# Two attention stages of a fused Trainium2 kernel: scores issued first in a block, one product piece per block, taps moved behind

## Chip, cores, metric

The kernel runs on one core of a Trainium2 chip. The metric is the device time of one execution in microseconds (us). The engines are TensorE (PE), VectorE (DVE), ScalarE (ACT), GpSimd (POOL) and SyncE (SP), which issues most transfers.

## What is computed

A first block (hybrid attention, then a recurrent mixer, each with a feed-forward network) and a second one of two layers, over 512 tokens of width 1024. The change touches the attentions. The first has eight heads of dilated attention (units 0 to 3, two heads each) and four heads of differential attention (units 4 to 7), whose output is normalized per head:

```
attn = p[:, :, 0] - lam * p[:, :, 1]
return jnp.einsum('bhqk,bkhe->bqhe', attn, vf)
...
ob = rms_norm(ob, b_sub_norm) * (1.0 - lam_init)
```

A layer of the second block has four branches over one input projection: chunked attention with a table of relative positions (units 0 and 1), attention over latents with rotary positions (units 2 and 3), attention with a forget gate, whose logits get `F[t] - F[s]`, a running sum over the tokens (units 4 and 5), and a causal depthwise convolution of 31 taps over 256 channels, followed by a layer norm. The gated sum of the four branches goes into the output projection.

## The kernel before, in words

All weights come as 470 slabs of 128x1024 f32. SP fetches a slab into a ring of three (`fetch`), ACT rounds it to `w_hi` (L841), POOL subtracts for `w_lo` (L1829), and TensorE makes each product of three passes: high by high, low by high, high by low (L395 to L397). A slab is 24 such matmuls of 128x512. An operand made on the chip is split in the same way: ACT takes the high half (L889), DVE the low half (`take_low`, L1250).

The attention runs in blocks of 128 queries, four to a unit, numbered n through the units. A block is taken through these steps: `scores` (PE L459, two lanes, banks 0 and 1), the min over the shifted scores (DVE L1323), the exponential (`rise`, ACT L896), the weighing by the reciprocal of the sum (`weigh`, DVE L1333 and L1345; in units 4 to 7 with lambda, L1340), `turn` (PE transposes, L472), `unturn` (the turned tile copied back, ACT L886 or DVE L1352), and per unit `mix` (PE L489, weighted values). In the first attention, units 4 to 7 end with `submean` and `subnorm` (reciprocal L1459, a product, high and low half).

Every engine walks the same list of steps, which `attention_steps` writes (L259 to L293) once for the first attention (`steps0`) and once for the layers of the second (`steps2`). An engine takes its part of each step in the list's order; semaphores hold it where its input isn't there. In iteration n the list has, in this order: turn, mix if a unit is complete, unturn (all of block n−3, `LAG` at L22), a unit's end, the fill for n, score of block n, weighing of block n−1, the second fill for n. The fill is product work of other parts: in the first attention the query and key units (`qk`) and value units (`vb`), each of two 24-matmul pieces of 256 columns (`token_unit`, L498), and the first output products (`out`); in the second the latents, the d inputs, keys, values and queries of the latent attention, the heads of the forget attention and the gated products (`fill2`, L336, and the lists behind it). The second fill holds the taps of the convolution (c = 0 on DVE at L1744, c = 1 on ACT and POOL) and the forget gate's steps, from the gather and back through several transfers to `sums`, a scan over the tokens (L1731), a sign (L1733) and eight small transfers into the tile `aug` (L1999 and L2000). Block 16's score waits for the last of these:

```
                                if a % NB == 0:
                                    T.wait_ge(scaled, ("c_head", L, 4 + c))
                                    T.wait_ge(scaled, ("c_head", L, 6 + c))
                                    T.wait_ge(l_aug, L)
```

The latents' norm is a root, a reciprocal of 128x512 (L1670), a product (L1677) and the halves (`latent_parts`); the rotary step is `rope` (L1680 on). A part 1 of the latents belongs to keys and values, a part 0 of two slabs to the queries. Behind the attention come gated products with the convolution's mean, variance and norm among them (`conv`, from L1768 on DVE).

Of the kernel before, what the change touches and what calls it, by code (L numbers as in the profile page):

```python
# [11 lines left out]
ALU = mybir.AluOpType  # L12
ACT = mybir.ActivationFunctionType

P = 128
# [5 lines left out]
NPAIR = 3  # L21
LAG = 3  # L22
# [97 lines left out]
def program(nc, x_in, small_in, fixed_in, heads_in, rel_in, pos_in, out):  # L120
# [3 lines left out]
    with ctx:  # L124
# [125 lines left out]
        y = {}  # L250
# [8 lines left out]
        def attention_steps(stage, units, fill=(), vfill=(), extra=None):  # L259
            n_blocks = NB * units  # L260
            at_block, after_block = {}, {}
            for lists, where in ((fill, at_block), (vfill, after_block)):
                for items, n0, n1 in lists:
                    for i, item in enumerate(items):
                        where.setdefault(n0 + i * (n1 - n0) // len(items), []).append(item)
# [24 lines left out]
            for i, stage_ in enumerate(later):  # L290
                steps += (extra or {}).get(n_blocks + LAG + i, [])
                steps.append(stage_)
# [8 lines left out]
        def turn_bank(stage, n, k):  # L301
# [6 lines left out]
        vb_banks = {(0, 0): 6, (0, 1): 6, (1, 0): 5, (1, 1): 6}  # L308
        before0 = {19: [("vb", (0, 0))], 21: [("qk_turn", 7), ("vb", (0, 1))], 23: [("vb", (1, 0))], 25: [("vb", (1, 1))],
                   1: [("qk_turn", 2)], 2: [("qk", (3, 1))], 0: [("qk", (3, 0))], 3: [("qk_root", 3)]}  # L310
        for p in range(4, 8):
            n = 4 * p - 12
            before0[n] = [("qk", (p, 0))]
            before0[n + 1] = [("qk_turn", p - 1)]
            before0[n + 2] = [("qk", (p, 1))]
            before0.setdefault(n + 3, []).insert(0, ("qk_root", p))
        norm0 = [[("qk_norm", p)] for p in range(3, 8)]
        out_banks = (5, 6, 0, 1, 2, 3, 4, 7)
        early0 = {27: [(0, 0, 4)], 28: [(1, 0, 4)], 29: [(0, 4, 5), (1, 4, 5)], 31: [(0, 5, 6), (1, 5, 6)],
                  32: [(2, 0, 4)], 33: [(3, 0, 4)], 34: [(2, 4, 6), (3, 4, 6)],  # L320
                  35: [(o, 6, 7) for o in range(4)] + [(4, 0, 7)], 36: [(5, 0, 7)]}
        for n, v in early0.items():
            before0[n] = [("out", a) for a in v]
        steps0 = attention_steps("first", 8, vfill=[(norm0[p - 3], 4 * p - 9, 4 * p - 8) for p in range(3, 8)], extra=before0)

        def qk_ready(n):
# [5 lines left out]
        mixed_list = [f for pair in zip([("forget", f) for f in forget], tap_list) for f in pair] + tap_list[len(forget):36]  # L332
        mixed_list = [f for f in mixed_list if f != ("forget", None)]
        fill2 = ([("latents", 0), ("d_input", 0), ("latent_norms", 0), ("d_input", 1), ("latent_parts", 1), ("rope", 0)]
                 + [("b_key", h) for h in range(4)] + [("latent_parts", 0), ("b_values", 0)]
                 + [("b_query", h) for h in range(4)])  # L336
        c_heads = {4: 1184, 6: 1440, 5: 1312, 7: 1568}
        steps2 = attention_steps("second", 6, [
            (fill2, 0, 8), ([("c_head", n) for n in (4, 6, 5, 7)], 8, 16),
            ([("gated", (0, c)) for c in range(8)], 16, 24), ([("gated", (1, c)) for c in range(4)], 24, 27)],  # L340
            [(mixed_list, 8, 16), (tap_list[36:], 16, 26)])
# [23 lines left out]
        def tensor(T):  # L365
# [132 lines left out]
            def token_unit(key, bank, c0, blocks, m):  # L498
# [5 lines left out]
                first = place[name, 0][0]  # L504
                wait_bank(bank)
                for b in blocks:
                    o = banks[bank][:, 256 * (b % 2):256 * (b % 2) + 256]
                    cols = slice(P * b, P * b + P)
                    for k in range(8):
                        slab, at = place[name, k]  # L510
                        wh, wl = w_hi[:, slab % NPAIR, at:at + 256], w_lo[:, slab % NPAIR, at:at + 256]
                        rh, rl = xr[k]
                        T.wait_ge(w_low, slab)
                        T.wait_ge(low, ("x", m, k))
                        pe.matmul(o, rh[:, cols], wh, start=(k == 0), stop=False)  # L515
                        pe.matmul(o, rl[:, cols], wh, start=False, stop=False)  # L516
                        last = pe.matmul(o, rh[:, cols], wl, start=False, stop=(k == 7))  # L517
                        done = [key] if b == blocks[-1] and k == 7 else []
                        if b == 3 and (name, k) in closes:
                            done.append(("slab", slab))  # L520
                        if done:
                            last.then_inc(*product.tick(*done))

            def qk(p, i):
                kind, half = pairs[p]
                bank = pair_banks[p][i]
                token_unit(("qk", p, i), bank, (0, 512, 1536, 2048)[kind] + 256 * half, (2 * i, 2 * i + 1), 0)
                free[bank] = (scaled, ("qk", p, i))
# [26 lines left out]
            for p, i in ((0, 0), (0, 1), (1, 0)):  # L555
                qk(p, i)
            qk_turn(0)
            qk(1, 1)
            qk(2, 0)
            qk_turn(1)  # L560
            qk(2, 1)
# [8 lines left out]
            for what, a in steps0:  # L570
# [4 lines left out]
                elif what == "vb":  # L575
                    half, i = a
                    bank = vb_banks[a]
                    token_unit(("vb",) + a, bank, 2560 + 256 * half, (2 * i, 2 * i + 1), 0)
                    free[bank] = (vec, ("vb",) + a)
# [82 lines left out]
            def hybrid(L):  # L662
# [29 lines left out]
                for what, a in steps2:  # L692
                    if what == "latents":
                        for n, c0 in enumerate([768, 896, 1024]):
                            bk = plain(("latent", L, n), c0)
                            free[bk] = (scaled, ("latent", L, n))
# [45 lines left out]
                    elif what == "d_input":  # L742
                        for half, c0 in ((0, 1956), (1, 2212)):
                            bk = plain(("d", L, a, half), c0 + P * a)
                            free[bk] = (vec, ("d", L, a)) if half == 0 else (act, ("d", L, a))
# [43 lines left out]

                T.wait_ge(taps, ("conv", L, 0, 30))  # L790
                T.wait_ge(pool, ("conv", L, 1, 30))
                wait_bank(4)
                sum_over(4, ("conv_mean", L), one256, [dcon[:, 0, :], dcon[:, 1, :]])
                free[4] = (vec, ("centred", L, 1))
                gated(1, 4)
                gated(1, 5)
                for c in range(2):
                    T.wait_ge(squared, ("conv", L, c))
                wait_bank(0)
                sum_over(0, ("conv_var", L), one256, [tmp[:, 1, :], tmp[:, 2, :]])  # L800
                free[0] = (rooted, ("conv", L))
                for c in range(6, 8):
                    gated(1, c)
                for c in range(8):
                    gated(2, c)
# [26 lines left out]
        def scalar(A):  # L832
# [89 lines left out]
            def qk(p, i):  # L922

                unit_weights(("qk", p), i)
# [29 lines left out]
            qk(0, 0)  # L954
            qk(0, 1)
            qk_root(0)
            qk(1, 0)
            qk_turn(0)
            qk(1, 1)
            qk_root(1)  # L960
            qk(2, 0)
            qk_turn(1)
            qk(2, 1)
            qk_root(2)
            for what, a in steps0:
# [6 lines left out]
                elif what == "vb":  # L972
                    half, i = a
                    unit_weights(("vb", half), i)
                    A.wait_ge(product, ("vb",) + a)
                    copy(att[:, 20 + 2 * i, 256 * half:256 * half + 256], banks[vb_banks[a]][:, 0:256],
                         ("vb",) + a, scale=rtok[:, 2 * i:2 * i + 1])
# [125 lines left out]
            def hybrid(L):  # L1103
# [18 lines left out]
                for what, a in steps2:  # L1122
                    if what == "latents":
                        for n in range(3):
# [971 lines left out]
```

## Time and profile before

| | |
|---|---|
| runs, median of 3 | 2961.24 us (2959.28 to 2962.02) |
| the profiled execution | 2963.23 us |
| its span on the page | 2961.4 us |
| PE busy | 2830.0 us, 96% |
| DVE, ACT, POOL busy | 1330.2, 1210.9, 1231.8 us (45, 41, 42%) |
| first attention | about 44 to 303 us |
| second attention, layer 0 and 1 | about 1331 to 1600 and 2161 to 2432 us |

The page gives the busy time of each engine and the granted clock of TensorE in slices. The views used below are the table of windows (busy time of each engine in a stretch, with the mean granted clock), the table of waits (an engine and line, the line it waited for), and the timeline of one engine's instructions.

### The profile page before, as it was taken

How to read it: one execution, taken by the hardware profiler on the slowest of the kernel's cores; microseconds unless marked ns; L12 is line 12 of the kernel's file. 1: busy time of each engine (PE TensorE's matmuls, PEld its weight loads, DVE VectorE, ACT ScalarE, POOL GpSimd, SP SyncE). 2: the span in 40 equal slices, each digit the busy share in tenths (PEclk: the TensorE clock that was granted, in tenths of full speed). 3: DMA queues.
4: the chain of work that ended last, by engine and by line, in shares of the span. 5: the costliest groups of instructions: out<-in, count | busy, mean ns of one | idle time of the engine just before them, and what ended most of it. 6: DMA issues, size and time to landing. Idle time of an engine off the chain costs nothing.

```text
span 2961.4 us, 32399 instructions
## 1 busy us (share of the span) xinstructions
PE 2830.0 (96%) x12934; PEld 2279.7 (77%) x12934; DVE 1330.2 (45%) x2094; ACT 1210.9 (41%) x1785; POOL 1231.8 (42%) x550
## 2 busy tenths in 40 slices
PE   8998999999879999998899999999998999999997
PEld 7775788888667888876577888888775678888886
DVE  4555651545865415434954352022239553531113
ACT  3554442434544324334574334233235743342331
POOL 3212344444454444432444444444433544444442
PEclk9999999999989999998999999999998999999999
DMA  4211233232222332322122323323321223233332
GB/s 144 80 61 54 86 100 93 93 107 89 75 65 92 100 100 93 100 92 80 37 72 86 100 93 100 95 98 100 93 93 37 67 70 106 93 100 94 99 97 74
DMA packets 73926, 259.21 MB, mean 88 GB/s; under 512 B 9184, under 2 KB 9184, under 8 KB 73776
## 3 DMA queue, kind: packets, MB, share of 16 engines
q1 hardware_dynamic: 71680, 251.79, 27.1%
q10 hardware_dynamic: 2096, 5.36, 0.5%
q8 instruction: 102, 1.67, 0.2%
q14 instruction: 48, 0.39, 0.0%
HBM read 254.95 MB, written 2.13 MB: 87 GB/s over the span
## 4 chain that ended last, share of the span: by engine, by line
PE 82%; DVE 10%; ACT 3%; issue 2%; POOL 2%; DMA 0%; DVEq 0%; ACTq 0%; POOLq 0%
PE ps L395 24%; PE ps L397 24%; PE ps L396 24%; PE ps L459 1%; PE ps L515 1%; PE ps L517 1%; PE ps L516 1%; POOL w_lo L1829 1%; DVE pbuf L1345 1%; PE ps L489 1%; DVE pbuf L1323 1%; PE ps L472 1%; PE ps L404 1%; PE ps L441 1%; PE ps L442 1%
## 5 line engine op out<-in xcount | busy, mean ns | idle before, releaser
L1829 POOL TENSOR_TENSOR w_lo<-raw,w_hi 128x1024 fp32r<-128x1024 f32 x470 | 1135.6, 2418 | 1562.9 <-ACT w_hi L841 1562.6
L395 PE MATMUL ps<-xs,w_hi 128*128 128x512 f32 x2176 | 859.8, 395 | 17.8 <-POOL w_lo L1829 11.0
L397 PE MATMUL ps<-xs,w_lo 128*128 128x512 f32 x2176 | 849.4, 390 | 0.0
L396 PE MATMUL ps<-xs,w_hi 128*128 128x512 f32 x2176 | 849.1, 390 | 0.0
L841 ACT ACTIVATE w_hi<-raw 128x1024 fp32r<-128x1024 f32 x470 | 494.5, 1054 | 711.1 <-PE ps L397 645.9
L395 PE MATMUL ps<-hid,w_hi 128*128 128x512 f32 x1320 | 524.2, 397 | 34.9 <-DVE hid L1250 12.8
L396 PE MATMUL ps<-hid,w_hi 128*128 128x512 f32 x1320 | 520.3, 394 | 0.0
L397 PE MATMUL ps<-hid,w_lo 128*128 128x512 f32 x1320 | 519.9, 394 | 0.0
L395 PEld LDWEIGHTS ps<-xs,w_hi 128*128 128x128 f32 x2176 | 410.4, 189 | 111.1 <-POOL w_lo L1829 13.8
L396 PEld LDWEIGHTS ps<-xs,w_hi 128*128 128x128 f32 x2176 | 410.2, 189 | 87.3 <-issue 3.4
L397 PEld LDWEIGHTS ps<-xs,w_lo 128*128 128x128 f32 x2176 | 409.8, 188 | 86.0
L395 PEld LDWEIGHTS ps<-hid,w_hi 128*128 128x128 f32 x1320 | 251.6, 191 | 93.3 <-DVE hid L1250 15.6
L397 PEld LDWEIGHTS ps<-hid,w_lo 128*128 128x128 f32 x1320 | 251.8, 191 | 53.0
L396 PEld LDWEIGHTS ps<-hid,w_hi 128*128 128x128 f32 x1320 | 251.8, 191 | 52.4 <-issue 0.5
L1296 DVE TENSOR_TENSOR ps<-ps,rt 128x512 f32<-128x512 f32 x182 | 126.6, 698 | 338.9 <-PE ps L397 338.3
L1284 DVE TENSOR_TENSOR hT<-ps,hT 128x512 f32<-128x512 f32 x96 | 66.0, 687 | 338.8 <-PE ps L397 338.8
L1265 DVE SCALAR_TENSOR_TENSOR xs<-hT,small,xs 128x512 fp32r<-128x512 f32 x64 | 111.1, 1735 | 162.9 <-ACT xs L865 162.8
L1024 ACT ACTIVATE tmp<-ps,small 128x512 f32<-128x512 f32 x96 | 74.9, 780 | 219.3 <-DVE ps L1296 219.3
L1250 DVE TENSOR_TENSOR hid<-tmp,hid 128x512 fp32r<-128x512 f32 x120 | 85.2, 711 | 131.3 <-ACT hid L889 131.3
L896 ACT ACTIVATE pbuf<-pbuf,tiny 128x128 f32<-128x128 f32 (+3 forms) x160 | 88.7, 556 | 115.1 <-DVE tiny L1323 114.8
L889 ACT ACTIVATE hid<-tmp 128x512 fp32r<-128x512 f32 x128 | 80.6, 631 | 100.9 <-DVE tmp L1521 88.0
L1219 ACT ACTIVATE tmp<-tmp 128x512 f32<-128x512 f32 x64 | 40.5, 632 | 199.0 <-DVE tmp L1805 199.0
(209 smaller groups left out, 2622.4 us busy)
## 6 DMA issues: line engine op xcount, KB each, us to landing
raw<-in_weights SPq DMA_DIRECT2D x470, 512.0 KB, 3.4
hT<-in_x ACTq DMA_DIRECT2D x4, 512.0 KB, 9.4
btab<-in_rel SPq DMA_DIRECT2D x8, 256.0 KB, 3.7
out<-tmp ACTq DMA_DIRECT2D x8, 256.0 KB, 2.8
btab<-in_heads SPq DMA_DIRECT2D x6, 256.0 KB, 3.7
tmp<-in_heads SPq DMA_DIRECT2D x6, 256.0 KB, 3.7
common<-in_fixed ACTq DMA_DIRECT2D x1, 642.0 KB, 13.0
small<-in_small ACTq DMA_DIRECT2D x1, 368.5 KB, 4.6
```

The costliest lines, as they stand in the source:

```text
L395: pe.matmul(banks[bank][:], wh, rh, start=(k == 0), stop=False)
L396: pe.matmul(banks[bank][:], wh, rl, start=False, stop=False)
L397: last = pe.matmul(banks[bank][:], wl, rh, start=False, stop=(k == len(specs) - 1))
L841: ac.activation(w_hi[:, n % NPAIR, :], raw[:, n % NRAW, :], ACT.Copy).then_inc(*w_high.tick(n))
L889: ac.activation(dst, src, ACT.Copy).then_inc(*high.tick(event))
L896: ac.activation(pbuf[:, i % 6, 0:w], pbuf[:, i % 6, 0:w], ACT.Exp, bias=tcol(3 * i), scale=-1.0, accum_out=tcol(3 * i + 1)).then_inc(*rise ...
L1024: ac.activation(tmp[:, 4 + j % 6, :], banks[j % 6][:], ACT.Identity, bias=small[:, bc + ch:bc + ch + 1], scale=small[:, wc + 3 * ch + 2:wc ...
L1250: ve.tensor_tensor(pair[1], src, pair[0].bitcast(F32), ALU.subtract).then_inc(*low.tick(event))
L1265: ve.scalar_tensor_tensor(out=lo, in0=hT[:, c, :], scalar=col(gname, g0 + c), in1=hi.bitcast(F32), op0=ALU.mult, op1=ALU.subtract).then_in ...
L1284: ve.tensor_tensor(hT[:, o, :], banks[bank][:], hT[:, o, :], ALU.add).then_inc(*resid.tick(event, ("chunk", m, o)))
L1296: ve.tensor_tensor(banks[bank][:], banks[bank][:], rt[:], ALU.mult).then_inc(*scaled.tick(event))
L1829: gp.tensor_tensor(w_lo[:, n % NPAIR, :], raw[:, n % NRAW, :], w_hi[:, n % NPAIR, :].bitcast(F32), ALU.subtract).then_inc(*w_low.tick(n))
```

## The change

The lag falls from 3 to 2, and an iteration now has the order score, weighing, a unit's end, the fill beside it, turn, mix, unturn, the fill behind it:

```
-LAG = 3
+LAG = 2
...
             for n in range(n_blocks + LAG):
                 due, later = later[:1], later[1:]
+                if n < n_blocks:
+                    steps.append(("score", n))
+                if 0 <= n - 1 < n_blocks:
+                    steps.append(("weigh", n - 1))
+                steps += due
+                steps += beside.get(n, [])
                 if n >= LAG:
                     steps.append(("turn", n - LAG))
...
                     steps.append(("unturn", n - LAG))
                     if (n - LAG) % NB == NB - 1:
                         late = (n - LAG) // NB
-                steps += due
-                steps += at_block.get(n, [])
-                steps += (extra or {}).get(n, [])
-                if n < n_blocks:
-                    steps.append(("score", n))
-                if 0 <= n - 1 < n_blocks:
-                    steps.append(("weigh", n - 1))
-                steps += after_block.get(n, [])
+                steps += (behind or {}).get(n, [])
```

A `qk` or `vb` unit is issued in two pieces of 24 matmuls, each a step of its own, and the pieces are dealt to the blocks, one to most of them. Value units lie in blocks 10 to 13 and 22 to 26. At block 24, beside the end of unit 4, lies nothing. The output products start at block 27 as before.

For the second attention the lists are written out. The three latents are one to a block, the d inputs move from blocks 0 and 1 to 9, 10, 13 and 14, the forget steps run in blocks 8 to 15 with `sums` in 15 (before: 12), 26 taps run in blocks 16 to 25, and 36 (18 pairs) behind the attention, between the gated products, with the convolution's mean, variance and norm as steps behind them:

```
+        beside2 = {0: [("latent", 0)], 1: [("latent", 1)], 2: [("latent", 2)], 3: [("latent_norms", 0), ("rope", 0)],
+                   4: [("latent_parts", 1), ("b_key", 0), ("b_key", 1)], 5: [("latent_parts", 0), ("b_values", 0)],
+                   6: [("b_query", 0), ("b_query", 1)], 7: [("b_key", 2), ("b_key", 3)], 8: [("b_query", 2), ("b_query", 3)],
+                   9: [("d_input", (0, 0))], 10: [("d_input", (0, 1))], 11: [("c_head", 4)], 12: [("c_head", 6)],
+                   13: [("d_input", (1, 0))], 14: [("d_input", (1, 1))], 15: [("c_head", 5)], 16: [("c_head", 7)],
+                   25: [("gated", (1, 0)), ("gated", (1, 1))]}
+        for c in range(8):
+            beside2[17 + c] = [("gated", (0, c))]
+        behind2 = {}
+        for i, f in enumerate(forget):
+            if f:
+                behind2.setdefault(8 + i * 8 // len(forget), []).append(("forget", f))
+        for i, f in enumerate(tap_list[:26]):
+            behind2.setdefault(16 + i * 10 // 26, []).append(f)
+        steps2 = attention_steps("second", 6, beside2, behind2)
...
+        rest = tap_list[26:]
+        for i, (n, c) in enumerate([(1, c) for c in range(2, 8)] + [(2, c) for c in range(5)]):
+            steps2 += rest[max(0, 4 * i - 8):max(0, 4 * i - 4)] + [("gated", (n, c))]
+        steps2 += [("conv_mean", 0), ("gated", (2, 5)), ("conv_var", 0), ("gated", (2, 6)), ("conv_norm", 0), ("gated", (2, 7)),
+                   ("conv_out", 0)]
```

DVE in the second attention, at the key latents. Before, the reciprocal and the halves of the latents (L1670 to L1250) stand ahead of the rope's steps (L1296 to L1634) and of the next min (L1323):

```order
L1670 RECIPROCAL tmp<-tmp 128x512
L1677 SCALAR_TENSOR_TENSOR att<-att,small,tmp 128x512
L1250 TENSOR_TENSOR hid<-att,hid 128x512
L1296 TENSOR_TENSOR ps<-ps,rt 128x512
L1684 TENSOR_SCALAR tmp<-ps,small 4x512
L1631 TENSOR_TENSOR tmp<-ps,rp 32x512
L1632 TENSOR_TENSOR tmp<-ps,rp 32x512
L1634 TENSOR_TENSOR att<-tmp 32x512
L1323 ISA pbuf,tiny<-ps,tmp 128x384
```

The same place in the changed kernel, with its line numbers (L1308 is the rope's scaling, L1783 the table of relative positions, L1335 the min, L1357 the weighing, L1262 the low half):

```order
L1308 TENSOR_TENSOR ps<-ps,rt 128x512
L1693 TENSOR_SCALAR tmp<-ps,small 4x512
...
L1644 TENSOR_TENSOR att<-tmp 32x512
L1783 SCALAR_TENSOR_TENSOR tmp<-btab,common 128x512 x2
L1335 ISA pbuf,tiny<-ps,tmp 128x128
...
L1345 RECIPROCAL tiny<-tiny 128x1
L1357 TENSOR_SCALAR pbuf<-pbuf,tiny 128x512
...
L1679 RECIPROCAL tmp<-tmp 128x512
L1686 SCALAR_TENSOR_TENSOR att<-att,small,tmp 128x512
L1262 TENSOR_TENSOR hid<-att,hid 128x512
```

The rope's five steps, the table, two mins and the weighing have moved ahead of the latents.

DVE at the forget sums. Before, the scan stands between two taps (L1744), and mins of other blocks follow:

```order
L1744 SCALAR_TENSOR_TENSOR att<-att,small 128x504
L1731 SCALAR_TENSOR_TENSOR tmp<-ones,tmp 4x512
L1733 TENSOR_SCALAR tmp<-tmp 4x512
L1744 SCALAR_TENSOR_TENSOR att<-att,small 128x503
L1323 ISA pbuf,tiny<-ps,common 128x256
```

In the changed kernel it stands behind the weighing of block 14 and the scaling of the last head (L1634), and right ahead of block 16's min:

```order
L1357 TENSOR_SCALAR pbuf<-pbuf,tiny 128x384
L1634 SCALAR_TENSOR_TENSOR att<-ps,rt 128x512
L1760 SCALAR_TENSOR_TENSOR tmp<-ones,tmp 4x512
L1762 TENSOR_SCALAR tmp<-tmp 4x512
L1335 ISA pbuf,tiny<-ps,common 128x128
```

The sums lie three blocks later, with no block between them and the score that reads `aug`.

TensorE in the changed kernel at block 16: the last head's product (L420), the turn of block 13 (L495), and the score (L482) that waits for the transfers (`l_aug`):

```order
L420 MATMUL ps<-xs,w_lo 128x512
L495 MATMUL ps<-common,pbuf 128x128 [waits moved,weight]
L495 MATMUL ps<-common,pbuf 128x128
...
L482 MATMUL ps<-att 128x128 [waits least,l_aug]
L482 MATMUL ps<-att 128x128 [waits least]
L482 MATMUL ps<-aug 128x128 x2
L418 MATMUL ps<-xs,w_hi 128x512 [waits vec]
```

Before, a gated product stood in front of that score, and the sums four blocks earlier.

## Rows read from the trace of the kernel before

**Rows 1.** The page: busy time of each engine, share, instructions.
```profile
PE 2830.0 (96%) x12934; PEld 2279.7 (77%) x12934; DVE 1330.2 (45%) x2094; ACT 1210.9 (41%) x1785; POOL 1231.8 (42%) x550
```
**Rows 2.** Windows: us, PE, PEld, DVE, ACT, POOL busy, PEclk, DMA share, GB/s.
```profile
400.00:500.00 100.00, 100.00 (x443) 82.81 (x442) 30.66 (x43) 30.94 (x37) 45.53 (x19) 1.00 0.32 98
82.05:178.30 96.25, 90.62 (x678) 74.16 (x677) 57.03 (x191) 58.05 (x128) 20.02 (x9) 1.00 0.22 69
178.30:300.00 121.70, 106.29 (x534) 79.12 (x535) 69.44 (x168) 58.47 (x119) 24.97 (x11) 0.93 0.17 55
226.69:230.10 3.41, 3.41 (x6) 1.77 (x7) 2.06 (x9) 1.31 (x4) 0.00 (x0) 0.50 0.71 231
243.76:254.00 10.24, 5.78 (x11) 2.90 (x12) 7.71 (x21) 4.46 (x11) 2.35 (x1) 0.50 0.17 53
```
**Rows 3.** Waits of PE, 44 to 303 us: us in total, times, longest.
```profile
PE ps L459 <- DVE tiny L1323: 9.0, 6, 5.0
PE ps L472 <- DVE pbuf L1340: 4.1, 5, 1.1
PE ps L395 <- DVE hid L1250: 2.8, 1, 2.8
...
PE ps L472 <- DVE pbuf L1345: 1.3, 4, 0.3
```
**Rows 4.** Timeline of DVE, a unit's end: start, us, line, operation.
```profile
241.20 3.35 DVE L1459 RECIPROCAL tmp<-tmp 128x512 f32<-128x512 f32 x1
...
246.03 0.69 DVE L1250 TENSOR_TENSOR hid<-tmp,hid 128x512 fp32r<-128x512 f32 x1 [0.70 <-ACT hid L889]
```
**Rows 5.** Windows of the second attention, layer 0 and 1.
```profile
1331.00:1480.00 149.00, 128.74 (x569) 93.15 (x567) 103.04 (x213) 71.06 (x153) 56.71 (x32) 0.93 0.19 61
1480.00:1600.00 120.00, 118.49 (x558) 87.55 (x557) 60.04 (x128) 74.13 (x112) 57.95 (x31) 1.00 0.24 75
1383.81:1394.05 10.24, 8.30 (x22) 4.71 (x20) 9.82 (x22) 7.19 (x18) 4.31 (x2) 0.50 0.17 51
2161.00:2310.00 149.00, 128.74 (x555) 92.66 (x553) 103.07 (x213) 71.18 (x153) 56.56 (x32) 0.91 0.20 61
```
**Rows 6.** Waits of PE, 1358 to 1600 us.
```profile
PE ps L472 <- ACT pt L886: 10.0, 7, 3.7
PE ps L395 <- DVE hid L1250: 4.8, 2, 4.4
```
**Rows 7.** Timeline of DVE, latents and rope of layer 0.
```profile
1377.46 3.34 DVE L1670 RECIPROCAL tmp<-tmp 128x512 f32<-128x512 f32 x1
...
1382.29 0.69 DVE L1250 TENSOR_TENSOR hid<-att,hid 128x512 fp32r<-128x512 f32 x1 [0.70 <-ACT hid L889]
1382.90 0.69 DVE L1296 TENSOR_TENSOR ps<-ps,rt 128x512 f32<-128x512 f32 x1
...
1385.83 0.68 DVE L1634 TENSOR_TENSOR att<-tmp 32x512 f32<-32x512 f32 x1
...
1394.09 1.27 DVE L1754 SCALAR_TENSOR_TENSOR tmp<-btab,common 128x512 f32<-128x512 f32 x2
...
1401.80 0.69 DVE L1250 TENSOR_TENSOR hid<-att,hid 128x512 fp32r<-128x512 f32 x1 [0.70 <-ACT hid L889]
1403.85 0.69 DVE L1250 TENSOR_TENSOR hid<-att,hid 128x512 fp32r<-128x512 f32 x1 [0.70 <-ACT hid L889]
```
**Rows 8.** Timelines of DVE and SP, and the transfers' landing time, at the sums.
```profile
1456.35 2.26 DVE L1731 TENSOR_TENSOR_SCAN tmp<-ones,tmp 4x512 f32<-4x512 f32 x1
...
1459.08 0.62 SPq L1999 DMA_DIRECT2D aug<-tmp  x1
...
1463.53 0.59 SPq L2000 DMA_DIRECT2D aug<-tmp  x1
...
aug<-tmp SPq DMA_DIRECT2D x16, 2.0 KB, 1.7
```
**Rows 9.** One line's instructions: the taps on DVE, min/median/max ns.
```profile
L1744 DVE SCALAR_TENSOR_TENSOR att<-att,small x60: 708/738/1740, 1429.9 to 2404.1; 128x511 f32<-128x511 f32 x2, 128x510 f32<-128x510 f32 x2, 128x509 f32<-128x509 f32 x2, 128x508 f32<-128x508 f32 x2
```

More of the change, by code:

```diff
@@ L257, in program, with attention_steps @@
                 y[layer, c] = pair
-        def attention_steps(stage, units, fill=(), vfill=(), extra=None):
+        def attention_steps(stage, units, beside, behind=None):
             n_blocks = NB * units
[L261 to L265, printed above, removed]
             steps, later = [], []
@@ L331, in program @@
         tap_list = [("tap", (c, n)) for n in range(31) for c in range(2)]
[L332 to L336, printed above, removed]
@@ L495, in u_to_y, with token_unit @@
                 return u
-            def token_unit(key, bank, c0, blocks, m):
+            def token_unit(key, j, bank, c0):
                 name, i = key[:-1], key[-1]
@@ L503, in token_unit @@
                         put((name, k), 256, ("attn_w_in", (0,), P * k, [(c0, c0 + 256)]), (name, 0))
[L504 to L522, printed above, removed]
@@ L524, in qk @@
-            def qk(p, i):
+                if j == 0:
+                    wait_bank(bank)
+                o = banks[bank][:, 256 * j:256 * j + 256]
+                cols = slice(P * (2 * i + j), P * (2 * i + j) + P)
+                for k in range(8):
+                    slab, at = place[name, k]
+                    wh, wl = w_hi[:, slab % NPAIR, at:at + 256], w_lo[:, slab % NPAIR, at:at + 256]
+                    rh, rl = xr[k]
+                    T.wait_ge(w_low, slab)
+                    T.wait_ge(low, ("x", 0, k))
+                    pe.matmul(o, rh[:, cols], wh, start=(k == 0), stop=False)
+                    pe.matmul(o, rl[:, cols], wh, start=False, stop=False)
+                    last = pe.matmul(o, rh[:, cols], wl, start=False, stop=(k == 7))
+                    done = [key] if j and k == 7 else []
+                    if i and j and (name, k) in closes:
+                        done.append(("slab", slab))
+                    if done:
+                        last.then_inc(*product.tick(*done))
@@ L554, in tensor @@
             free[4] = (vec, "etok")
[L555 to L561, printed above, removed]
+            for what, a in before0:
+                if what == "qk":
+                    qk(*a)
+                elif what == "qk_turn":
+                    qk_turn(a)
             def y_first(k):
@@ L575, in tensor @@
                 elif what == "vb":
[L576 to L579, printed above, removed]
+                    half, i, j = a
+                    bank = vb_banks[half, i]
+                    token_unit(("vb", half, i), j, bank, 2560 + 256 * half)
+                    free[bank] = (vec, ("vb", half, i))
                 elif what == "score":
@@ L692, in hybrid @@
                 for what, a in steps2:
[L693 to L696, printed above, removed]
+                    if what == "latent":
+                        bk = plain(("latent", L, a), (768, 896, 1024)[a])
+                        free[bk] = (scaled, ("latent", L, a))
                     elif what == "latent_norms":
@@ L1712, in hybrid @@
                         gated(*a, 8 * a[0] + a[1])
+                    elif what == "conv_mean":
+                        for c in range(2):
+                            V.wait_ge(mean, ("conv_mean", L))
+                            if c:
+                                V.wait_ge(pool, ("conv", L, 1, 30))
+                            ve.tensor_tensor(dcon[:, c, :], dcon[:, c, :], banks[4][:], ALU.subtract).then_inc(
+                                *vec.tick(("centred", L, c)))
+                    elif what == "conv_norm":
+                        r = tmp[:, 4, :]
+                        V.wait_ge(rooted, ("conv", L))
+                        chain(ve.reciprocal(r, r))
+                        for c in range(2):
+                            V.wait_ge(step)
+                            V.wait_ge(squared, ("conv", L, c))
+                            ve.tensor_tensor(dcon[:, c, :], dcon[:, c, :], r, ALU.mult).then_inc(*vec.tick(("normed", L, c)))
+                    elif what == "conv_out":
+                        for c in range(2):
+                            take_low(y[L, 6 + c], tmp[:, 8 + c, :], ("y", L, 6 + c))
                     elif what == "forget":
@@ L1937, in sync @@
             until("va")
-            for p in range(3):
-                until(("qk", p))
+            for what, a in before0:
+                if what == "qk":
+                    until(("qk", a[0]))
             first_tables(0)
```

273 lines of the change are left out of this document (124 added, 149 removed).

## The prediction

> **What bounds the kernel now.** The page's totals come first: TensorE is busy for 2830.0 us of a span of 2961.4, and no other engine for half of it [rows 1]. With the same work the change can therefore win only from the 131 us in which TensorE stands, or from what half the clock costs it. The table of windows says where that is. Outside the attentions, as at 400 to 500 us, TensorE has no gap: 443 products in 100 us, so .226 us for one of 128x512, 5.42 for a slab of 24, and half of it, 2.7, for a piece of 24 with 256 columns [rows 2]. In the first attention it stands 5.6 us from 82 to 178 (units 0 to 3) and 15.4 from 178 to 300 (units 4 to 7) [rows 2]. In the second it stands 20.3 us in the 149 from block 0 on and 1.5 in the 120 behind them, and nearly the same in layer 1 [rows 5].
>
> The clock comes with it. A mean grant of .93 over 121.7 us, with levels 1.00 and .50 alone (2.4 and 1.2 GHz), is 17 us at the half: the 10.24 and a 3.41 of the rows, and one more 3.41. TensorE is busy for 5.78 in the long one and all through the short ones [rows 2], 12.6 in all, half of which full clock would have saved: 6.3. In the second attention .93 is 21 us at half and .91 is 27; at the .81 busy share of the row there [rows 5] that is a loss of 8 in layer 0. Layer 1's stretches are less busy, about .74 (my estimate between the two shares of the rows), so 10.
>
> Then the waits of TensorE. In the first attention the largest is a score that waits for an earlier min to free its bank, 9.0 us in 6, the longest 5.0. Turns wait 4.1 for the weighing with lambda and 1.3 for the plain one, and the output product waits 2.8 at the end [rows 3]. In the second, turns wait 10.0 for a turned copy (L886), and the latents' products 4.8 for VectorE's low halves (L1250) [rows 6]. Turns are late there because VectorE is: it is busy for 103 of the 149 us [rows 5], with taps among the attention's own steps.
>
> **First attention, units 0 to 3.** Per block there is now one score, one piece of 2.7 and one turn that is two blocks old; before, a unit of two pieces sat in one block of two. The score ahead of the piece lets the min, rise and weighing run under the piece. I take the 5.6 us down to 1.7: the turns' wait for the weighing stays (1.3 [rows 3]), with .4 of rounding in places I can't see. Gain **3.9**. The bounds are all of it, 5.6, and a loss of 2, if a turn that is a block younger waits in half of the 16 blocks as long as in the longest of those waits, .3.
>
> **First attention, units 4 to 7.** The end of a unit (root, reciprocal, product, high and low half) holds VectorE from 241.20 to 246.72, 5.5 us [rows 4]. Before, it stood ahead of the score and its min. Now it stands behind the score and weighing of its block, and so ahead of the turn's copy and the next min. Units 4, 5 and 6 pass through it. The next score but one needs the bank that this min frees: 5.5, the two mins (.4 each, an estimate: narrower than the .69 of a 512-column step [rows 4]), and about .5 for the copy make 6.9, against one piece of 2.7 and about .6 of score and turn. That is 3.6 three times, **10.7**. With .6 for the last mix and 1.5 of small waits (an estimate, a third of the 4.1 for the lambda weighing [rows 3]) it is 12.8 idle, where 15.4 was. The wait of 2.8 at the end [rows 3] goes, since output products of other units lie there. The clock still drops behind such waits, 6.0 by the same kind of stretches. So 18.8 for 21.7: gain **2.9**. Bounds: all of the 15.4 less the small waits, and nothing.
>
> **Second attention, per layer.** Before: 20.3 + 1.5 idle and 8 of clock is 29.9; layer 1, with 10, is 31.6. The taps' crowding in blocks 8 to 15 goes: 26 taps lie in blocks 16 to 25 and 36 behind the attention, so about 11 us of turns and bank waits go with the 10.0 [rows 6]. What is late next:
> - Block 4. The rope's steps now stand on VectorE ahead of block 4's min and of the key latents. Behind the rope's product VectorE needs 3.6 for them (from 1382.90 to 1386.51), 1.75 for the table (1.27) and the block's mins, 1.2 for weighing (the mins and the weighing estimated from their widths), and 5.5 for reciprocal to low half (1377.46 to 1382.98) [rows 7]: 12.1. TensorE has about 1.0 beside it, a turn and a score. Idle **11.1**, where this wait was 4.8 in all [rows 6].
> - Block 6. The query products need the other latents: mins and weighing 1.6 (an estimate, as in block 4) and again 5.5, 7.1 after the score against 3.3 of products, so **3.8**; their second half is ready 2.05 later (1401.80 to 1403.85 [rows 7]), with .7 of products between, **1.35**.
> - Block 16. The forget sums move from block 12 to 15, and the score of block 16 waits for them. Behind the last head's product come its scaling (.69, as the L1296 of [rows 7]), the scan 2.26, a sign, and eight transfers issued in line from 1459.08 to 1463.53, the last landing 1.7 later [rows 8]. From 1456.35 to 1465.23 is 8.9, so 9.6 with the scaling; .6 of turn lies beside it: **9.0**. Before, this chain had four blocks to run in, and cost nothing.
> - The conv variance, 1.3, about what it was.
>
> Together 26.6. The clock: three long waits, each followed by a half-clock stretch, 7.1 by the same .81 share over 17.5 us. 33.7 per layer, a loss of 3.8 and 2.1: **5.9**. Bounds per layer: 4 better, if half of block 4's wait is covered by a score that runs ahead; 9 worse, if half the clock lasts on.
>
> The 36 taps behind the attention cost nothing in this sum: between two gated products VectorE has three scalings (.69), one more step of that size and two taps (.74 each) [rows 7, 9], 4.3 us for 6.8 of TensorE (30 products). If the taps run at the longest of their row, 1.74, it is 6.3, still covered. The table loads on the SP queue and the slab fetches between the forget hops keep their number; the products at 400 us show slabs arriving without a gap, so nothing is added for them.
>
> **Sum.** −3.9 −2.9 +5.9 = −0.9, against the profiled execution of 2963.2 us: 2962.3. The median of the runs is 2.0 below the profiled one, so **2960**. A measurement of this kernel can tell about .2%, 6 us, from no change. By the bounds the likeliest case alone spans 2954 to 2967.
>
> **The clock, and a rule on it.** At 243.76 the granted clock is .50 for 10.24 us, right behind a 5.0 us wait [rows 2, 3]. The Trainium skill, "TensorE: Matmul & The Clock Gate", section "What's actually happening", has it that "the default state is throttled, and activity releases the throttle". The trace agrees in sign: the .50 stretches lie behind waits and none lies in 400 to 500 us [rows 2]. The rule speaks against a change that gathers small waits into a few long ones; taken strictly, the sum would be that of the first rival.
>
> **Rivals.**
> 1. *Slower, 2972.* Idle time is as forecast, but in the second attention half the clock holds from block 4's wait on to block 8's products, about 20 us, and again for 10.24 behind block 16's wait [rows 5]. At the .81 share (less the 11 of waiting) TensorE loses some 13 per layer in place of 7.1: +12 in all. It decides if more than 20 us of a layer are at .50 behind block 4. For it: the 149 us of before already hold 21 and 27. Against: before's stretches have many waits close together, and these are few. Chance .25.
> 2. *Faster, 2948.* The three waits behind the units' ends vanish, because the score and min of a block now come ahead of the fill and of the end's work, and TensorE has a queue of pieces and turns that reach over 5.5 us. Then 10.7 of idle and most of the 6 of clock go too: −3.9 −15.7 +5.9 = −13.7, less the 2.0. For it: the largest wait of before, 9.0 for the min [rows 3], is just what the new order addresses. Against: at block 24 no piece stands beside the end at all. Chance .30.
> 3. *Slower, 2969.* The tail becomes VectorE's. In the row of the taps one takes .74 mostly, but up to 1.74 [rows 9], beside GpSimd's own share of the taps. If scalings stretch as the longest tap did, to 1.6 times, VectorE needs 7.3 in a step of 6.8, and a step's result is late by .5 in nine steps of each layer: +9. The Trainium skill, "SBUF — State Buffer", section "Who interferes with whom", tells of a port pair that VectorE and GpSimd share as an exclusive lock; the longest tap agrees with it, but no row names the lock. Chance .07.
>
> That the change doesn't do what it says can be set aside: the order of rows shows the scores ahead, the sums at block 15 and the taps behind. The likeliest is the sum, .38.
>
> **Chances.** Faster by over .2% (below 2955.3): rival 2 and a little of the sum's case, .35. Slower (above 2967.2): rivals 1 and 3, .30. Within: .35. Cases of both signs hold most of the chance; the range reaches to both, with the bounds a little beyond: 2944 to 2974.
>
> **What would show it.** Right: in the trace of the changed kernel TensorE waits about 9 us at the score of block 16 for the last small transfer, about 11 at the first key products for L1262 (the low half), and 3 to 4 behind three units' ends; no turn waits for L886's copy in blocks 8 to 15; idle in the first attention falls by about 6. Wrong: no wait over 5 us at block 16 or block 4 (then the second attention gains, and the time is below 2950); or a mean grant below .90 over the second attention (rival 1); or products between the gated steps that wait for VectorE (rival 3).

## The result, and the profile after

The changed kernel takes 2977.17 us (median of 4 runs, 2974.41 to 2978.86) where the kernel before takes 2960.8: a ratio of 1.0055, 95% interval 1.0037 to 1.0072. It is 16 us slower. The forecast was 2960, no change; the time lies outside the range of 2944 to 2974. The profiled execution is the fastest of the four, 2974.41 with a span of 2972.6, so its trace shows 11 us more than before's (2963.23). The other 5 us of the 16 stand in no trace of this kernel. One execution of the last edit below, at 3637.95 us and a mean granted clock of .73, is a slow one and is left out of that edit's median.

The first question is where the 11 us are. ScalarE rounds the slabs in the same order in both kernels, so the start of the same rounding, behind the first attention, is a common mark. The row of each kernel, before first, then changed:

```profile
350.70 1.05 ACT L841 ACTIVATE w_hi<-raw 128x1024 fp32r<-128x1024 f32 x1
```
```profile
357.40 1.05 ACT L855 ACTIVATE w_hi<-raw 128x1024 fp32r<-128x1024 f32 x1
```

The first attention is 6.7 us longer, where 6.8 shorter was forecast. The starts of the same roundings further on, in us:

| the same rounding, behind | before | changed | longer so far |
|---|---|---|---|
| the first attention | 350.70 | 357.40 | 6.7 |
| the recurrent mixer | 927.60 | 932.23 | 4.6 |
| layer 0 of the second attention | 1744.44 | 1753.91 | 9.5 |
| layer 1 | 2565.03 | 2576.10 | 11.1 |

By these marks layer 0 is 4.8 longer and layer 1 is 1.6, 6.4 together, where 5.9 was forecast. Between the two attentions lies the mixer, which the change doesn't touch and which became 2.1 shorter (last section). So 6.7 + 6.4 − 2.1 is the whole difference of the traces, and the second attention came as predicted in sum.

Windows of the changed kernel, in the columns of [rows 2]; the first two answer to those rows, the third is a stretch in and behind the first wait below, and the last two answer to [rows 5]:

```profile
82.05:178.30 96.25, 89.86 (x646) 74.52 (x647) 55.58 (x185) 55.49 (x123) 21.29 (x9) 0.95 0.20 66
178.30:306.70 128.40, 111.05 (x556) 84.28 (x555) 75.15 (x174) 64.39 (x126) 26.20 (x11) 0.91 0.15 52
85.37:92.20 6.83, 5.55 (x23) 4.27 (x24) 4.38 (x13) 3.76 (x8) 1.10 (x1) 0.50 0.27 79
1337.00:1486.00 149.00, 125.34 (x565) 92.62 (x565) 80.59 (x213) 63.12 (x144) 35.89 (x15) 0.90 0.19 59
1486.00:1606.00 120.00, 118.51 (x560) 89.96 (x559) 65.77 (x113) 67.08 (x99) 63.38 (x34) 1.00 0.24 75
```

VectorE fell from 103 to 81 us in the first 149 of the second attention, as moving the taps had to make it, and yet TensorE stands longer there: 23.7 us for 20.3. In the first attention TensorE stands 6.4 us from 82 to 178 where it was to be 1.7, and 17.4 behind that where it was to be 12.8; and the clock, full before [rows 2], is now .95 from 82 to 178. Who is waited for stands in the waits of TensorE, first attention (44 to 310 us):

```profile
PE ps L482 <- DVE tiny L1335: 7.3, 3, 3.8
PE ps L418 <- DVE hid L1262: 5.8, 2, 2.9
PE ps L560 <- DVE tmp L1415: 5.2, 2, 5.1
PE ps L560 <- ACT tmp L1009: 3.6, 1, 3.6
PE ps L537 <- ACT att L900: 2.4, 3, 1.6
...
PE ps L512 <- ACT pt L900: 0.7, 1, 0.7
```

and second attention, layer 0 (1335 to 1606 us):

```profile
PE ps L418 <- issue: 11.4, 1, 11.4
PE ps L482 <- DMA aug<-tmp: 8.1, 1, 8.1
PE ps L418 <- DVE hid L1262: 4.2, 2, 3.8
PE ps L512 <- DVE pt L1364: 1.2, 1, 1.2
```

Of the first list, the three waits behind the units' ends are there (3.3 and 3.8 of L1335, 2.9 of L1262). The key latents' wait at block 4 is the line of 11.4, for which the table names no releaser (issue); the low half ends right before that product starts, at 1377.04 and 1377.14:

```profile
1376.35 0.69 DVE L1262 TENSOR_TENSOR hid<-att,hid 128x512 fp32r<-128x512 f32 x1 [0.70 <-ACT hid L903]
```

Two lines of the first list have no term in the forecast: the turn of a query unit (L560) waits 5.1 us for the unit's scaling (L1415), and another turn 3.6 for a root (L1009). Before, such turns waited .5 in all:

```profile
PE ps L538 <- DVE tmp L1401: 0.5, 2, 0.3
```

**The first wait.** VectorE of the changed kernel around it: start, us, line, operation, and in brackets its own idle time and what ended it.

```profile
81.12 0.29 DVE L1335 CUSTOM_DVE_ANT_0 pbuf<-ps,btab 128x128 f32<-128x128 f32 x1 [4.16 <-DMA btab<-in_heads]
...
85.61 0.25 DVE L1410 RECIPROCAL tiny<-tiny 128x16 f32<-128x16 f32 x1 [3.03 <-ACT tiny L949]
85.90 1.29 DVE L1415 TENSOR_TENSOR tmp<-ps,tiny 128x512 f32<-128x512 f32 x2
```

The very first min stands 4.16 us for its table of distances, a transfer, and the reciprocal of query unit 2 stands in line behind it. The root that this reciprocal needs is on ScalarE behind the exponential of the same block, which needs the min. SP's timeline says why the table is late:

```profile
62.86 14.43 SPq L1918 DMA_DIRECT2D raw<-in_weights  x3
77.33 0.91 SPq L1929 DMA_DIRECT2D btab<-in_heads  x2
```

The table is issued behind the slabs of the query units, and a slab is issued when a place in the ring comes free. Before, it was no earlier (issued at 77.88), but there the reciprocal of unit 2 stood ahead of the first min on VectorE and ran at 77.80:

```profile
77.80 0.25 DVE L1396 RECIPROCAL tiny<-tiny 128x16 f32<-128x16 f32 x1 [0.28 <-ACT tiny L932]
...
83.46 0.28 DVE L1323 CUSTOM_DVE_ANT_0 pbuf<-ps,btab 128x128 f32<-128x128 f32 x1
```

Putting the score first put the min, with its unseen transfer, ahead of the unit's norm on VectorE and, through its root, on ScalarE, which both keep to the list's order.

**The second wait.** TensorE and ScalarE of the changed kernel at block 23:

```profile
206.79 1.10 PE L427 MATMUL ps<-tmp,ones 128*128 128x512 f32 x2
211.46 1.81 PE L560 MATMUL ps<-common,tmp 128*128 128x128 f32 x8 [3.57 <-ACT tmp L1009]
```
```profile
206.58 1.28 ACT L910 ACT_TABLE_LOAD   x1
207.88 0.72 ACT L910 ACTIVATE pbuf<-pbuf,tiny 128x512 f32<-128x512 f32 x1
...
209.42 1.28 ACT L1009 ACT_TABLE_LOAD   x1
210.72 0.69 ACT L1009 ACTIVATE tmp<-ps,tiny 128x512 f32<-128x512 f32 x1
```

The mean of unit 4 (L427) goes into bank 7, which the turn of query unit 7 needs too. The mean comes first now, and holds the bank until its root, which ScalarE takes behind two exponentials (one of the two is shown) and a table load on either side of them.

### The profile page after: what moved, and what is told of

Same layout as the page of the kernel before. It is cut to its first block, busy times and chain, and to the rows that moved or that the text cites. A ratio compares the mean times of both kernels' runs of the same rounds, so it can differ in the third digit from the quotient of the medians.

```text
span 2972.6 us, 32386 instructions
## 1 busy us (share of the span) xinstructions
PE 2828.2 (95%) x12934; PEld 2286.1 (77%) x12934; DVE 1354.6 (46%) x2094; ACT 1209.6 (41%) x1781; POOL 1244.1 (42%) x550
## 3 DMA queue, kind: packets, MB, share of 16 engines
q1 hardware_dynamic: 71680, 251.79, 26.6%
## 4 chain that ended last, share of the span: by engine, by line
PE 86%; DVE 6%; ACT 3%; issue 2%; POOL 1%; DMA 1%; SPq 0%; DVEq 0%; ACTq 0%; POOLq 0%
PE ps L418 25%; PE ps L420 25%; PE ps L419 25%; PE ps L482 3%; PE ps L512 2%; PE ps L537 1%; PE ps L495 1%; PE ps L539 1%; PE ps L538 1%; POOL w_lo L1837 1%; PE ps L427 1%; PE ps L464 1%; PE ps L465 1%; PE ps L466 1%; ACT w_hi L855 0%
## 5 line engine op out<-in xcount | busy, mean ns | idle before, releaser
L420 PE MATMUL ps<-xs,w_lo 128*128 128x512 f32 x2176 | 850.5, 391 | 0.0
L420 PE MATMUL ps<-hid,w_lo 128*128 128x512 f32 x1320 | 519.4, 393 | 0.0
L420 PEld LDWEIGHTS ps<-xs,w_lo 128*128 128x128 f32 x2176 | 410.6, 189 | 86.7
L420 PEld LDWEIGHTS ps<-hid,w_lo 128*128 128x128 f32 x1320 | 251.4, 190 | 53.1
L1308 DVE TENSOR_TENSOR ps<-ps,rt 128x512 f32<-128x512 f32 x182 | 126.4, 697 | 274.9 <-PE ps L420 274.4
L1296 DVE TENSOR_TENSOR hT<-ps,hT 128x512 f32<-128x512 f32 x96 | 66.0, 687 | 336.8 <-PE ps L420 336.8
L1262 DVE TENSOR_TENSOR hid<-tmp,hid 128x512 fp32r<-128x512 f32 x120 | 85.6, 714 | 136.7 <-ACT hid L903 136.7
```

What stands on the lines that cost most here:

```text
L420: last = pe.matmul(banks[bank][:], wl, rh, start=False, stop=(k == len(specs) - 1))
L1262: ve.tensor_tensor(pair[1], src, pair[0].bitcast(F32), ALU.subtract).then_inc(*low.tick(event))
L1308: ve.tensor_tensor(banks[bank][:], banks[bank][:], rt[:], ALU.mult).then_inc(*scaled.tick(event))
```

## The experiments

Each is the changed kernel with the edit shown; the times are medians, beside 2961 for the kernel before in the same comparisons.

**Second attention alone** (the first attention's step list as before, lag 3, with a unit's two pieces side by side):

```
-        steps0 = attention_steps("first", 8, beside0)
+        steps0 = old_steps("first", 8, vfill=[...], extra=beside0)
```

> The changed kernel with the first attention in the order of before (lag 3, units whole, old lists), so the second attention's change alone. Theory A (the trace of the changed kernel: the first attention is 6.7 us longer, the second 4.8 and 1.6): 2967, 6.4 over before, with waits of 11.4 and 8.1 in each layer. Rival B (the loss lies in the second attention, the first only shifts it): 2974 or more.

Measured: 2968.53, ratio 1.0027 (1.0016 to 1.0038). By the marks the first attention is .4 over before's, layer 0 is 4.1 longer and layer 1 1.6; the waits of 11.4 and 8.1 are unchanged. A holds: the second attention costs 6 to 8, and the rest of the 16 comes with the order of the first attention. (By the traces that rest is 6.7 less the 2.1 of the mixer, by the medians 8 to 9.)

**Tables early:**

```
             until("va")
+            first_tables(0)
             for what, a in before0:
                 if what == "qk":
                     until(("qk", a[0]))
-            first_tables(0)
```

> The changed kernel with the first unit's tables issued on SP ahead of the slabs of the query and key units. Theory A (the first min waits for its table until 81.1, and the norm of unit 2 stands behind it on VectorE and ScalarE): TensorE's wait of 5.1 at the turn of unit 2 goes to under .5, and the half clock from 86 to 94 us with it (3.7): 2968, 9 less than the changed kernel. Rival B (the root of unit 2 is late by itself, for two table loads of 1.28 on ScalarE): the wait stays over 2, 2974.

Measured: 2966.32, ratio 1.0022 (1.0013 to 1.0032), 11 less than the changed kernel. VectorE no longer waits for the table, and the turn of unit 2 comes on the heels of the products:

```profile
77.80 0.28 DVE L1335 CUSTOM_DVE_ANT_0 pbuf<-ps,btab 128x128 f32<-128x128 f32 x1
...
81.50 0.25 DVE L1410 RECIPROCAL tiny<-tiny 128x16 f32<-128x16 f32 x1 [3.21 <-ACT tiny L949]
```
```profile
82.00:94.00 12.00, 11.77 (x83) 9.23 (x83) 7.49 (x23) 6.68 (x14) 2.79 (x2) 1.00 0.15 52
82.00:178.00 96.00, 93.98 (x705) 77.15 (x706) 59.00 (x194) 57.69 (x126) 22.69 (x11) 1.00 0.23 73
```

```profile
PE ps L560 <- DVE tmp L1415: 0.3, 2, 0.2
```

The wait is .3 in place of 5.2, and the clock from 82 to 94 is full. From 82 to 178 TensorE stands 2.0 us: that is the 1.7 that the prediction left to units 0 to 3. By the marks the first attention is 8.0 shorter than the changed kernel's; 5 of these are the wait, and I put the other 3 down to the clock: the stretch from 85.37 to 92.20, half of whose 5.55 us of products full clock would have saved, is gone. A holds. The reciprocal still waits 3.2 us for ScalarE here, so B's late root is there, but it no longer holds TensorE.

**Turn of unit 7 ahead of the mean**, with the value piece that stood beside it:

```
+                steps += (ahead or {}).get(n, [])
                 steps += due
...
-        beside0[23] = [("qk_turn", 7), last_vb[1]]
+        ahead0 = {23: [("qk_turn", 7), last_vb[1]]}
```

> The changed kernel with the turn of query unit 7 and a value piece ahead of unit 4's mean in block 23 in place of behind it. Theory A (the turn waits for bank 7, which the mean holds until its root, and the root stands behind an exponential and two table loads on ScalarE): the wait of 3.6 goes, with about 2 of half clock behind it: 2972, 5 less than the changed kernel. Rival B (the mean comes some 4 us later, and the wait returns at the scores behind unit 4's end): within 2 of 2977, and that wait grows from 3.3 to 5 or more.

Measured: 2966.72, ratio 1.0020 (1.0011 to 1.0029), 10 less, twice what A gave; the profiled execution, the slowest of the ten, shows 3.4 less in the first attention. The wait for L1009 is gone from its list and those behind the units' ends did not grow:

```profile
PE ps L483 <- DVE tiny L1336: 7.1, 2, 3.8
PE ps L419 <- DVE hid L1263: 5.8, 2, 3.0
PE ps L561 <- DVE tmp L1416: 5.0, 2, 4.8
```

A's mechanism holds. Its size is less sure: 3.4 by that trace, 10 by the medians, and on top of the early tables (next run) 4.7 by the marks and 6 by the medians; 4 to 6 is what I take, and why the medians show more here is open.

**Both edits of the first attention:**

> The changed kernel with the two edits in the first attention alone (tables early on SP, turn of unit 7 ahead of the mean). Theory A (these two waits and the half clock behind them are the whole of what the prediction missed; without them the first attention gains about the 6.8 that it gave, and the second loses about 6): 2957 to 2964, the first attention 5 to 8 shorter than before's. Rival B (a part of the loss has another cause, in the order or the lag): 2966 or more.

Measured: 2960.23, ratio 1.0001 (.9992 to 1.0010). The mark behind the first attention, to compare with 350.70 and 357.40 above:

```profile
344.62 1.05 ACT L856 ACTIVATE w_hi<-raw 128x1024 fp32r<-128x1024 f32 x1
```

and the window of units 4 to 7, where [rows 2] had 15.4 us of standing and a clock of .93:

```profile
178.00:300.00 122.00, 108.31 (x529) 82.00 (x526) 76.37 (x165) 62.18 (x121) 27.84 (x12) 0.92 0.15 52
```

TensorE stands 13.7 us in it, where 12.8 was forecast (it reaches some 6 us further into the work than the window before). The first attention is 6.1 shorter than before's (forecast 6.8), the second 4.1 and 1.6 longer (forecast 3.8 and 2.1), and the time is the 2960 of the forecast. A holds: these two waits and the clock behind them are what the prediction missed in the first attention.

**Sums at block 13:**

```
-                behind2.setdefault(8 + i * 8 // len(forget), []).append(("forget", f))
+                behind2.setdefault(13 if f == "sums" else 8 + i * 8 // len(forget), []).append(("forget", f))
```

> The changed kernel with the forget sums behind block 13 in place of 15. Theory A (block 16's score waits for scan, sign and eight transfers): the wait of 8.1 goes to under 1 in both layers, with some 2 of half clock behind each: 2957, 20 less than the changed kernel. Rival B (the sums would stall VectorE at block 13, since the transfer back is not there yet, and its mins with it): 5 less at most, and a wait of a score for a min at blocks 14 or 15.

Measured: 2956.98, ratio .9986 (.9976 to .9996), 20 less, the 2957 of A. The waits of layer 0:

```profile
PE ps L418 <- issue: 11.4, 1, 11.4
PE ps L418 <- DVE hid L1262: 4.2, 2, 3.8
PE ps L512 <- DVE pt L1364: 1.2, 1, 1.2
```

The wait at block 16 is gone and nothing took its place. The position of this one step, in the two layers, is worth more than all that the change lost.

**Key latents ahead of the rope:**

```
-        3: [("latent_norms", 0), ("rope", 0)], 4: [("latent_parts", 1), ("b_key", 0), ("b_key", 1)],
+        3: [("latent_norms", 0), ("latent_parts", 1), ("rope", 0)], 4: [("b_key", 0), ("b_key", 1)],
```

> The changed kernel with the key latents' steps ahead of the rope in block 3 in place of behind it in block 4. Theory A (VectorE is idle for 5.9 us beside the rope's product, and the rope's steps, table, mins and weighing then push the latents back): the wait of 11.4 at the first key products goes to about 1, a wait of about 2.5 comes at block 5's score, and 2 of half clock go, per layer: 2958, 19 less than the changed kernel. Rival B (the same work stands ahead of block 5's score, and the wait moves there): 6 less, with a wait over 6 at that score.

Measured: 2967.14, ratio 1.0019 (1.0010 to 1.0029), 10 less: between A and B. The waits of layer 0:

```profile
PE ps L482 <- DMA aug<-tmp: 8.1, 1, 8.1
PE ps L418 <- DVE hid L1262: 5.3, 2, 4.5
PE ps L495 <- ACT pt L900: 4.0, 1, 4.0
PE ps L418 <- issue: 1.4, 1, 1.4
```

The wait of 11.4 went to 1.4, as A had it, but 4.0 came back: at the turn of block 2, not at block 5's score as either theory said. On ScalarE the turned copy (L900) stands behind three copies of the rope, which wait for VectorE's rope steps.

**All taps under the attention:**

```
-        for i, f in enumerate(tap_list[:26]):
-            behind2.setdefault(16 + i * 10 // 26, []).append(f)
+        for i, f in enumerate(tap_list):
+            behind2.setdefault(16 + i * 10 // 62, []).append(f)
...
-        rest = tap_list[26:]
+        rest = []
```

> The changed kernel with all 31 pairs of taps in blocks 16 to 25, six taps to a block, and none behind the attention. Theory A (taps among an attention's own steps make VectorE late, which is what the change takes out of the second attention): turns or scores wait again in blocks 16 to 25, 2 to 5 us per layer: 2981 to 2987. Rival B (VectorE has room beside the gated products, and the move of 18 pairs bought nothing): 2977 within 2, no new wait.

Measured: 2985.35, ratio 1.0083 (1.0066 to 1.0100), 8 more. From 1475 to 1600 us TensorE stands 4.7 us (1.5 in the 120 us of the changed kernel above), with a new wait for ScalarE, whose L1127 is the sigmoid of a gate:

```profile
1475.00:1600.00 125.00, 120.31 (x561) 90.29 (x560) 87.43 (x135) 76.30 (x116) 80.72 (x47) 0.99 0.23 72
```
```profile
PE ps L418 <- ACT tmp L1127: 2.2, 1, 2.2
PE ps L512 <- DVE pt L1364: 1.9, 1, 1.9
```

A holds in size; the waits are at a product and a mix, though, and not at the turns and scores that it named. The tap pairs that moved behind the attention bought something; they were not the loss.

**The four edits together** (tables, turn, sums, latents), and then with the rope behind the turned copies in block 3's iteration and two value pieces a block earlier:

```
-        3: [("latent_norms", 0), ("latent_parts", 1), ("rope", 0)],
+        3: [("latent_norms", 0), ("latent_parts", 1)],
...
-        behind2 = {}
+        behind2 = {3: [("rope", 0)]}
...
-        beside0[25], beside0[26] = last_vb[2:3], last_vb[3:]
+        beside0[24], beside0[25] = last_vb[2:3], last_vb[3:]
```

> The changed kernel with four edits together: tables early on SP, turn of unit 7 ahead of the mean, sums at block 13, key latents ahead of the rope. Theory A (four separate waits, which add): 11 + 5 + 20 + 10 less than 2977, 2931. Rival B (they share half-clock stretches or the waits move on): 2942 or more, still below both kernels if the sums and latents alone add (2947).

> As the four edits together, with the rope behind the turned copies of block 3 and the value pieces of blocks 25 and 26 one block earlier, beside unit 4's end. Theory A (the score behind unit 4's end waits 3.3 for want of a piece beside it, and the turn of block 2 waits 4.0 behind the rope's copies on ScalarE): 2.5 less in the first attention, 1 less per layer: 4 to 5 below the four edits. Rival B (the piece is missed where it was): the same as the four edits.

Measured: 2929.92, ratio .9894 (.9880 to .9909), and 2920.82 (three executions), ratio .9868 (.9851 to .9884). The first is near the 2931 of A. That sum took 5 for the turn of unit 7; with the 10 that its own run measured it would be 2926, so the four add up to about 4 us. The second took 9 more, where 4 to 5 was expected (by the marks 4 in the first attention and 3 in each layer); its longest wait in the second attention, layer 0 (1330 to 1610 us):

```profile
PE ps L483 <- DVE tiny L1336: 3.1, 1, 3.1
...
```

The score that waits 3.1 here is block 5's, the one that theory A of the key latents had named. The changed order with its waits taken out beats both kernels, that of before by some 40 us.

**The changed kernel again:**

> The changed kernel again, nothing edited, on the chip of the run above. Both theories: 2977 within 2, the second attention 4 to 8 longer than before's over both layers. What it tells: how far the first attention's length moves from run to run by the granted clock alone (6.7, 8.7 and 10.5 over before's in three profiles with the same first attention).

Measured: 2976.29, ratio 1.0051 (1.0037 to 1.0065), with the first attention again 6.7 over before's. The two profiled executions of this kernel took nearly the same time, 2974.41 and 2974.38 us; others took up to 2979.21 and left no trace. So the run doesn't settle how far the first attention moves from one execution to the next.

The lag of 2 by itself was not tried, and neither was the bank wait at 109 us (L900, 1.6).

## Why the prediction was wrong, step by step

- **The likeliest case and its sum.** Wrong in one term, the first attention: −6.8 given, +6.7 measured, beyond its own bounds, which left room for a loss of 2. Slips in the working changed little: 5.5, .8 and .5 make 6.8 and not 6.9; 20.3, 1.5 and 10 make 31.8 and not 31.6; and rival 2's −15.7, if it is the 10.7 and 5 of clock, leaves out the 2.9 that the sum already had.
- *Units 0 to 3, gain 3.9.* Once the tables are early, TensorE stands 2.0 us there for 5.6 before: right by .3. The step that failed is a term that the sum put at nothing. The prediction let the min run under the piece, as VectorE's work alone, and never asked what else the first min needs. The table loads on SP were dismissed in a sentence on the second attention; in the first, the table on SP was what the new order ran into. It cost 5.1 us of waiting and, by the experiment, some 3 of clock.
- *Units 4 to 7, gain 2.9.* The three waits behind the units' ends were given as 3.6 each and are 3.3, 3.8 and 2.9; the last mix as .6 and is .7. Two parts were wrong: the turn of unit 7 behind the mean (3.6) had no term but the 1.5 of small waits, though bank 7 is shared, and cost 4 to 6 with the clock behind it; and the wait of 2.8 at the end was said to go, and is still there (the 5.8 of L1262 is 2.94 and 2.82).
- *Second attention, +5.9.* Right in sum: +6.4 in the trace, +5.7 in the run with both first edits. Part of that is luck, since two errors cancel in layer 0: TensorE stands 25.2 us (23.7 and 1.5 in the windows above) where 26.6 was given, and half the clock costs about 8.6 (rows below) where 7.1 was given. Block 4 was given as 11.1 and is 11.4; block 6 as 3.8 and is 3.8, its second half 1.35 and is .4. Block 16 was given as 9.0 and is 8.1: the scan took 1.20 in place of 2.26. The turns' waits of [rows 6] went as forecast, and 1.2 came at a mix, while the 1.3 at the conv variance didn't come.
- *The rivals.* Rival 1, half clock, had its stretches right: layer 0 is at .50 for 20.5 us from block 4's wait on and for 10.24 at block 16 (rows below). But its price did not come: part of them lies inside the waits, where nothing is lost, TensorE is busy for 17.2 us of them, and half of that is 8.6, not 13. The loss of clock that made the kernel slower lies in the first attention, where idle time rose by only 1.3 us (25.6 from 44 to 303 before, 26.9 from 44 to 310 now), and most of the 6.7 is therefore clock. Rival 2 did not come: the units' ends kept their waits. Rival 3 did not come: no product between the gated steps waited for VectorE. (Its 1.6 times for the longest tap is 2.4 by [rows 9], 1740 to 738 ns.)
- *The rule of the clock.* The trace bears it out in sign, but "behind" a wait was a misreading, of before's trace too. The clock falls inside the wait: at 85.37, in a wait from 81.57 to 86.65, and before at 243.76, in the 5.0 us wait that ended at 247.12. With the wait of 5.1 gone, the clock is full there.

The stretches of the changed kernel at half the clock in layer 0 of the second attention:

```profile
1368.78:1382.43 13.65, 5.29 (x17) 3.65 (x17) 8.11 (x14) 7.43 (x15) 2.37 (x1) 0.50 0.11 30
1389.26:1396.09 6.83, 6.09 (x14) 4.10 (x14) 5.49 (x15) 4.08 (x10) 0.00 (x0) 0.50 0.00 0
1464.36:1474.60 10.24, 5.83 (x18) 4.48 (x19) 1.64 (x8) 1.94 (x5) 0.21 (x1) 0.50 0.01 1
```

## What to carry to other kernels

When a step is issued earlier, list everything that its first instance needs, transfers too, and look up when each is issued on its own queue: the one that was never waited for is the one that nobody has timed. An in-order engine passes such a wait on to work that has nothing to do with it, here to a norm on VectorE and through a root on ScalarE. A chain that ends in small transfers should be started as early as its input allows: two blocks were worth 20 us over two layers.

## What was not expected of the hardware

The granted clock follows more than idle time. The first attention has the same steps in the changed kernel, in the run with the sums moved and in that with the latents moved. From 44 us to the start of the same rounding (283.4, 286.6 and 284.8 us) TensorE stands 24.0, 23.9 and 23.7 us; yet by the mark behind the attention it is 6.7, 10.5 and 8.7 over before's. These are single executions, the first the fastest of its four, the others the slowest and next to slowest of their ten, so whether the program or the execution makes the difference is not shown.

In the recurrent mixer, untouched by the change, the grant over the same 60 us is .89 before and .94 in the changed kernel, though TensorE stands longer there in the changed one, 14.3 us for 10.4. The row before, then changed:

```profile
830.00:890.00 60.00, 49.58 (x188) 38.85 (x187) 38.18 (x34) 24.79 (x34) 30.53 (x15) 0.89 0.23 70
```
```profile
837.00:897.00 60.00, 45.73 (x186) 35.70 (x184) 39.57 (x36) 26.01 (x36) 30.47 (x15) 0.94 0.22 70
```

With that go the 2.1 us that came back there. A sum of waits did not give differences of 2 to 4 us of this kind, and no experiment here looked for what sets them.
